# A three-layer transformer on one core: attention results ahead of centring, norm sums by pairs, and the third feed-forward begun on the unnormalised stream

## The chip, the cores and the metric

The kernel runs on one core of one Trainium2 chip. The metric is the device time of one execution in microseconds. The kernel before took 1150.14 us (median of 3 runs, 1149.94 to 1151.73).

## The reference, cut to what matters

Three layers work on one sequence of 256 tokens with width 1024, in float32. The first two are alike (`first_block`), the third is another kind (`second_block`):

```python
# first_block, twice
h = rmsnorm(x, norm_mix[l]);  proj = h @ w_in[l]
# ... attention over selected keys, HGRN recurrence, gates ...
x = x + merged @ w_out[l]
h = rmsnorm(x, norm_ffn[l])
g, u = jnp.split(h @ w_ffn_in[l], 2, axis=-1)
x = x + (jax.nn.silu(g) * u) @ w_ffn_out[l]

# second_block, once
h = rms_norm(x, mix_pre_g[i]) * (1.0 + sc1) + sh1
y = hybrid_mixer(h, ...)   # concat(attention, silu(layer_norm(conv))) @ w_o
x = x + g1 * rms_norm(y, mix_post_g[i])
h = rms_norm(x, ffn_pre_g[i]) * (1.0 + sc2) + sh2
y = swiglu_ffn(h, w_ffn_in[i], w_ffn_out[i])
x = x + g2 * rms_norm(y, ffn_post_g[i])
```

The feed-forward is 2816 wide, which makes 11 slices of 256. A norm's factor `rsqrt(mean(x*x))` belongs to one token, so it can be multiplied in before or after a product over the features; the shift `sh2` can be multiplied with the weights by itself and added afterwards.

## The kernel before, in words

**Units.** All weights pass through TensorE as a list of units, mostly 1024 x 256 weights (1 MB). A unit passes four queues. SyncE loads it into `raw` (6 slots, in the order of the list; a slot is free when `w_lo` of the unit six before is written). ScalarE writes `w_hi`, its rounded high part (`split` on ScalarE), VectorE writes `w_lo`, the rest (`split` on VectorE), each into one of 3 slots, which is free when TensorE has done the unit three before. TensorE then makes three products for each chunk, high by high, high by low and low by high, so as to keep float32's accuracy. The activations are split in the same way (`h_hi`, `h_lo` and so on). All four queues run in program order: `tick()` on ScalarE or VectorE steps to the next unit and splits the one three ahead, `split_ahead()` splits alone, `step()` steps alone. Where these calls stand among the other work is written by hand, and so is TensorE's order.

**Norm sums.** `square` on ScalarE writes the squares of `x` into `h_norm` (8 chunks of 128 features by 256 tokens; each `square` does a pair of chunks). `squares_folded` on VectorE folds 8 chunks to 4 and then to 2 with three additions of 128x512, and `norm_sum` on TensorE sums the two chunks over the partitions with a matrix of ones (`A[0]` gets it). This happens between the first and the second unit of a layer's mixer and its feed-forward. Norms are numbered 0 and 2 (mixers of the first two layers), 1 and 3 (their feed-forwards), 4 (third mixer), 5 (third feed-forward). Unit "ix0", "ix1", "aq0" are a first layer's first three.

**Third mixer's end.** The attention of query tile 1 ends in VectorE's generator `attend`: the inverse row sums, then for two halves of the heads `y = values x inverse` (L1794), then `ya_lo` of both halves (L1798), with `ya_hi` on ScalarE between. The convolution's layer norm runs beside it: the folded sum, the centring `cv - mean` (L2261, released by `c_mu`), squares, a second sum on TensorE (L1038), `rstd`, then `conv_out_hi` and `conv_out_lo` by chunk. The four output units "tout0" to "tout3" (`w_o`) multiply `ya` and `conv_out` into the four banks `A`; bank j holds token tile j // 2 and column half j % 2. `tout0` waits for `ya_lo` of the first half.

**Third feed-forward's start.** When tout3 is done, ScalarE squares each bank (`out_squares`), makes each token tile's factor (`out_factor`), VectorE multiplies with the gain row (`gained_out`, L2279) and adds to the stream (`finished`, L2286), which lies token-major in `x_tm`. ScalarE squares the new stream (`x_squares`), and its factor `rs_x` is multiplied in for all four parts of `x_tm` on VectorE and ScalarE. TensorE turns the result into `A` (`turn_h`, L821), VectorE applies gain and shift, ScalarE makes `h_hi` and VectorE `h_lo`, and TensorE does the first unit, "gate0", pair by pair (`high_parts_first`, L840 to L845). Then come up0, gate1, up1, down0, gate2, up2, down1 and so on. A down unit needs `gu_lo` of its slice, made from `silu(gate) * up`.

Units whose factor and shift are applied afterwards are called `shifted`: they multiply `xs_hi`/`xs_lo`, the gained stream with the shift in two more columns (258 in all). In the kernel before those are the third mixer's first two units.

Of the kernel before, what the change touches and what calls it, by code (L numbers as in the profile page):

```python
# [143 lines left out]
def shifted(u):  # L144
    return u[1] == 2 and u[2] in ("gate0", "val0")
# [48 lines left out]
def build(nc, a, out):  # L194
# [87 lines left out]
    gain_row = [at("mixer_gain_row", [P, D], F32, 159), at("ffn_gain_row", [P, D], F32, 163)]  # L282
    gain_dram = nc.dram_tensor("gain_rows_in_dram", (2, D), F32, kind="Internal").ap()
    xn = at("x_tm_normed", [P, 4, 512], F32, 167)
# [95 lines left out]
    n_fold = Event("norm_squares_folded")  # L380
# [8 lines left out]
    x_scaled, x_sq2, x_ms2 = Event("x_tm_scaled_by_act", 2), Event("x_tm_squares"), Event("x_tm_mean_squares")  # L389
    p_part, x_rs, x_norm, h_turned = Event("out_part", 3), Event("x_tm_rstd"), Event("x_tm_normed_set", 2), Event("h_turned", 4)  # L390
# [123 lines left out]
    def _(sp):  # L514
# [7 lines left out]
        for m in range(2, len(UNITS)):  # L522
# [24 lines left out]
    def _(pe):  # L547
# [33 lines left out]
        def turned(hi, lo, x_h, x_l, k0, first, part):  # L581

            for j in range(4):
# [4 lines left out]
                if part and j < 3:  # L588
                    mm.then_inc(part.sem, 1)
            return mm  # L590

        def stream(count, before=None, between=None):

            for _ in range(count):
# [50 lines left out]
                elif kind == "tout":  # L645
# [3 lines left out]
                    pe.wait_ge(*(y_lo.at(0, name) if name < 2 else c_lo.at(0, k0 + 1)))  # L649
                    mm = turned(hi, lo, y_h, y_l, k0, name == 0, p_part if name == 3 else None)  # L650
# [54 lines left out]
        def norm_sum(ni):  # L705
            pe.wait_ge(*n_fold.at(ni))
# [108 lines left out]
        def turn_h(half):  # L815

            pe.wait_ge(*x_norm.at(0, half))
            pe.wait_ge(*x_scaled.at(0, half))
            for k in range(4 * half, 4 * half + 4):
                for t in range(NT):  # L820
                    mm = pe.transpose(A[k // 2][:, T * (k % 2) + P * t:T * (k % 2) + P * t + P],  # L821
                                      xn[:, 2 * t + half, P * (k % 4):P * (k % 4) + P], ident)
                if k % 2:
                    mm.then_inc(h_turned.sem, 1)

        def high_parts_first():
# [3 lines left out]
            pe.wait_ge(*lo_at(m))  # L830
            for e, c in BANKS[m][1]:
# [3 lines left out]
            for j in range(4):  # L835
                pairs = [(n, k) for n in range(2) for k in (2 * j, 2 * j + 1)]
                pe.wait_ge(*n_hi.at(NTH_NORM[5], j))
                for n, k in pairs:
                    out, ws = bank(m)[:, T * n:T * n + T], (slice(None), k, slice(P * n, P * n + P))
# [1558 lines left out]
```

## Time and profile before

| | |
|---|---|
| median of 3 runs | 1150.14 us |
| the profiled execution's own time | 1151.75 us |
| its span, first to last instruction | 1149.7 us |
| TensorE busy | 1113.0 us, 97% |
| VectorE busy | 861.6 us, 75% |
| ScalarE busy | 622.6 us, 54% |
| mean granted TensorE clock | 0.992 |

The span is what the trace shows; 2.05 us of the profiled execution lie outside it. PE is TensorE, PEld its weight loads, DVE VectorE, ACT ScalarE, SPq the DMA queue that SyncE issues to. All ScalarE work carries the line of one helper, so it is told apart by its tiles.

### The profile page before, as it was taken

How to read it: one execution, taken by the hardware profiler on the slowest of the kernel's cores; microseconds unless marked ns; L12 is line 12 of the kernel's file. 1: busy time of each engine (PE TensorE's matmuls, PEld its weight loads, DVE VectorE, ACT ScalarE, POOL GpSimd, SP SyncE). 2: the span in 40 equal slices, each digit the busy share in tenths (PEclk: the TensorE clock that was granted, in tenths of full speed). 3: DMA queues.
4: the chain of work that ended last, by engine and by line, in shares of the span. 5: the costliest groups of instructions: out<-in, count | busy, mean ns of one | idle time of the engine just before them, and what ended most of it. 6: DMA issues, size and time to landing. Idle time of an engine off the chain costs nothing.

```text
span 1149.7 us, 20164 instructions
## 1 busy us (share of the span) xinstructions
PE 1113.0 (97%) x8452; PEld 1065.2 (93%) x8452; DVE 861.6 (75%) x1357; ACT 622.6 (54%) x780; POOL 0.2 (0%) x4
## 2 busy tenths in 40 slices
PE   5999999999999999999999999999999988999997
PEld 5899999999999998999999999999998868999997
DVE  7997766777988877986767788898699966545444
ACT  7677465554444356584664644344588576334333
POOL 0000000000000000000000000000000000000000
PEclk9999999999999999999999999999999998999999
DMA  9646444747879554564346568796555154555520
GB/s 345 210 147 186 145 147 144 254 153 261 278 249 318 164 169 149 156 199 157 122 135 227 193 224 280 245 316 209 160 148 176 43 185 147 184 184 183 184 74 37
DMA packets 176394, 215.14 MB, mean 187 GB/s; under 512 B 5808, under 2 KB 157744, under 8 KB 176304
## 3 DMA queue, kind: packets, MB, share of 16 engines
q1 hardware_dynamic: 175616, 213.20, 56.8%
q8 instruction: 67, 1.10, 0.4%
q10 hardware_dynamic: 688, 0.66, 0.2%
q14 instruction: 23, 0.19, 0.0%
HBM read 212.79 MB, written 1.06 MB: 186 GB/s over the span
## 4 chain that ended last, share of the span: by engine, by line
PE 76%; DVE 17%; ACT 5%; issue 2%; DMA 1%; DVEq 0%; ACTq 0%
PE stream L552 16%; PE stream L554 16%; PE stream L553 16%; DVE w_lo L1583 6%; PE steps L552 6%; PE steps L553 6%; PE steps L554 6%; ACT w_hi L1054 2%; PE stream L636 1%; PE stream L638 1%; PE stream L637 1%; DVE conv_acc L2166 1%; PE steps L966 1%; PE stream L804 1%; DVE conv_acc L2180 1%
## 5 line engine op out<-in xcount | busy, mean ns | idle before, releaser
L1583 DVE TENSOR_TENSOR w_lo<-raw,w_hi 128x2048 fp32r<-128x2048 f32 (+2 forms) x178 | 401.3, 2265 | 175.4 <-ACT w_hi L1054 174.4
L1054 ACT ACTIVATE w_hi<-raw 128x2048 fp32r<-128x2048 f32 (+2 forms) x178 | 336.3, 1893 | 285.3 <-PE stream L554 247.7
L552 PE MATMUL stream<-h_hi,w_hi 128*128 128x256 f32 x1592 | 455.3, 286 | 3.3 <-DVE w_lo L1583 3.0
L553 PE MATMUL stream<-h_lo,w_hi 128*128 128x256 f32 x1592 | 450.4, 283 | 0.0
L554 PE MATMUL stream<-h_hi,w_lo 128*128 128x256 f32 x1592 | 450.4, 283 | 0.0
L552 PEld LDWEIGHTS stream<-h_hi,w_hi 128*128 128x128 f32 x1592 | 305.2, 192 | 7.8 <-DVE w_lo L1583 5.1
L553 PEld LDWEIGHTS stream<-h_lo,w_hi 128*128 128x128 f32 x1592 | 305.4, 192 | 1.4 <-issue 1.0
L554 PEld LDWEIGHTS stream<-h_hi,w_lo 128*128 128x128 f32 x1592 | 305.3, 192 | 0.0
L552 PE MATMUL steps<-gu_hi,w_hi 128*128 128x256 f32 x352 | 99.9, 284 | 0.2 <-DVE gu_lo L1885 0.2
L553 PE MATMUL steps<-gu_lo,w_hi 128*128 128x256 f32 x352 | 99.6, 283 | 0.0
L554 PE MATMUL steps<-gu_hi,w_lo 128*128 128x256 f32 x352 | 99.6, 283 | 0.0
L1853 DVE SCALAR_TENSOR_TENSOR ada_sum<-ada_raw,c_act,ada_sum 128x256 f32<-128x256 f32 x168 | 81.5, 485 | 6.0
L1054 ACT ACTIVATE gu_hi<-gu 128x512 fp32r<-128x512 f32 x33 | 20.9, 632 | 101.4 <-DVE gu L1881 101.4
L552 PEld LDWEIGHTS steps<-gu_hi,w_hi 128*128 128x128 f32 x352 | 67.5, 192 | 0.4 <-issue 0.4
L553 PEld LDWEIGHTS steps<-gu_lo,w_hi 128*128 128x128 f32 x352 | 67.5, 192 | 0.0
L554 PEld LDWEIGHTS steps<-gu_hi,w_lo 128*128 128x128 f32 x352 | 67.5, 192 | 0.0
L636 PE MATMUL stream<-w_hi,h_hi 128*128 128x512 f32 (+1 forms) x152 | 59.3, 390 | 1.7 <-DVE w_lo L1583 1.7
L638 PE MATMUL stream<-w_lo,h_hi 128*128 128x512 f32 (+1 forms) x152 | 58.1, 382 | 0.0
L637 PE MATMUL stream<-w_hi,h_lo 128*128 128x512 f32 (+1 forms) x152 | 58.0, 382 | 0.0
L1885 DVE TENSOR_TENSOR gu_lo<-gu,gu_hi 128x512 fp32r<-128x512 f32 x33 | 22.8, 692 | 23.0 <-ACT gu_hi L1054 23.0
L552 PE MATMUL stream<-x_gained_hi,w_hi 128*128 128x256 f32 x128 | 36.8, 287 | 0.9 <-DVE x_gained_lo L1632 0.9
L636 PEld LDWEIGHTS stream<-w_hi,h_hi 128*128 128x128 f32 x152 | 29.2, 192 | 7.7 <-DVE w_lo L1583 2.3
(367 smaller groups left out, 1620.0 us busy)
## 6 DMA issues: line engine op xcount, KB each, us to landing
raw<-in_w_ffn_in SPq DMA_DIRECT2D x66, 1024.0 KB, 5.7
raw<-in_w_in SPq DMA_DIRECT2D x54, 1024.0 KB, 5.4
raw<-in_w_ffn_out SPq DMA_DIRECT2D x33, 1024.0 KB, 5.1
ada_raw<-in_ada_w SPq DMA_DIRECT2D x24, 1024.0 KB, 6.4
raw<-in_w_out SPq DMA_DIRECT2D x8, 1024.0 KB, 5.1
raw<-in_w_proj_attn SPq DMA_DIRECT2D x8, 512.0 KB, 3.5
raw<-in_w_proj_hgrn SPq DMA_DIRECT2D x8, 512.0 KB, 4.5
raw<-in_w_o SPq DMA_DIRECT2D x4, 1024.0 KB, 4.9
```

Source lines behind the costliest of these rows:

```text
L552: pe.matmul(dst, w_h, x_h, start=start, stop=False, skip_group_check=True)
L553: pe.matmul(dst, w_h, x_l, start=False, stop=False, skip_group_check=True)
L554: return pe.matmul(dst, w_l, x_h, start=False, stop=stop, skip_group_check=True)
L636: pe.matmul(dst, h_h[:, k0 + k, ts], hi[:, k, :], start=k0 + k == 0, stop=False)
L637: pe.matmul(dst, h_l[:, k0 + k, ts], hi[:, k, :], start=False, stop=False)
L638: mm = pe.matmul(dst, h_h[:, k0 + k, ts], lo[:, k, :], start=False, stop=k0 + k == KC - 1)
L804: mm = pe.matmul(conv_bank[:, 0:T], diag[j], upad[:, 3, j:j + T], start=j == 0, stop=j == PE_TAPS - 1)
L966: mm = pe.matmul(level_bank(i)[:, c, :], kp[i % 2][:, c, :], qp[:, c, :].rearrange("p (n two h) -> p n two h", two=2, h=h)[:, :, 1, :], st ...
L1054: return act.activation(out_, in_, func, **kw)
L1583: tt(wl[m % SPL][:, 0:n], raw[m % RAW][:, 0:n], wh[m % SPL][:, 0:n].bitcast(F32), ALU.subtract)\
L1853: ins = stt(acc, w[:, k, :], cact[:, k:k + 1], acc, ALU.mult, ALU.add)
L1885: tt(gu_l[i % 2].rearrange("p c t -> p (c t)"), gu, gu_h[i % 2].rearrange("p c t -> p (c t)").bitcast(F32), ALU.subtract).then_inc(*lane.m ...
```

## The change

Four places are changed.

1. **Norms 0 and 2.** Four additions of 128x256, one for each pair of squares, replace the three of 128x512, and TensorE sums the four results as they come.
2. **Third mixer.** VectorE does both halves of `y` and `ya_lo` before the centring; a split (of tout1) moves from ahead of them to behind the centring. tout0 does its high parts first and waits for `ya_lo` only ahead of the rest.
3. **Third feed-forward.** gate0 and up0 become shifted units. TensorE turns the new stream itself (`turn_x2`), ScalarE and VectorE make `xs_hi` and `xs_lo` with the gain, and the token factor, spread on VectorE and turned on TensorE, comes afterwards. VectorE makes the normalised `h` from the turned stream (`third_normed`), ScalarE its high part; gate1 is the first unit that uses it. The splits of up0 and gate1 move ahead of the factor on VectorE, that of gate1 ahead of it on ScalarE, and those of up1 and later behind the normalised parts on both.
4. **Memory.** The second gain row moves to where `h_norm` lies, so SyncE's queue also waits for `ya_lo` there.

```diff
 def shifted(u):
-    return u[1] == 2 and u[2] in ("gate0", "val0")
+    return u[1] == 2 and (u[2] in ("gate0", "val0") or u[0] in ("gate", "up") and u[2] == 0)
...
             if m == UOUT[2] + 7:
                 sp.wait_ge(gains_out, 32)
                 sp.wait_ge(*a_pt.upto(2))
+                sp.wait_ge(*y_lo.upto(0))
...
+        def turned_high_first(hi, lo, x_h, x_l, low):
+            parts = [(j, k, slice(P * (j // 2), P * (j // 2) + P), slice(512 * (j % 2), 512 * (j % 2) + 512))
+                     for j in range(4) for k in range(2)]
+            for j, k, ts, ws in parts:
+                pe.matmul(A[j], x_h[:, k, ts], hi[:, k, ws], start=k == 0, stop=False, skip_group_check=True)
+                pe.matmul(A[j], x_h[:, k, ts], lo[:, k, ws], start=False, stop=False, skip_group_check=True)
+            pe.wait_ge(*low)
+            for j, k, ts, ws in parts:
+                mm = pe.matmul(A[j], x_l[:, k, ts], hi[:, k, ws], start=False, stop=False, skip_group_check=True)
+            return mm
...
         def norm_sum(ni):
-            pe.wait_ge(*n_fold.at(ni))
+            if ni in (0, 2):
+                for j in range(4):
+                    pe.wait_ge(*n_pair.at(ni // 2, j))
+                    mm = pe.matmul(A[0][:, 0:T], ones, hn[:, 2 * j, :], start=j == 0, stop=j == 3)
+                mm.then_inc(n_ms.sem, 1)
+                return
...
+        def turn_x2():
+            for j, t, chunks in ((1, 0, range(KC)), (2, 1, range(4)), (3, 1, range(4, KC))):
+                pe.wait_ge(*x2_new.at(0, j))
+                for k in chunks:
                     mm = pe.transpose(A[k // 2][:, T * (k % 2) + P * t:T * (k % 2) + P * t + P],
-                                      xn[:, 2 * t + half, P * (k % 4):P * (k % 4) + P], ident)
+                                      x_tm[:, 2 * t + k // 4, P * (k % 4):P * (k % 4) + P], ident)
...
             if b == 2:
-                turn_h(0)
-                turn_h(1)
+                turn_x2()
                 high_parts_first()
-                stream(3 * FS - 1)
+                turn_rstd()
+                stream(1)
+                stream(1, normed(5))
+                stream(3 * FS - 3)
...
-            for j in range(1, 4):
+            for j in range(3):
                 x_squares(j)
+            for j in range(4):
+                act.wait_ge(*x2_turned.at(0, j))
+                for k in (2 * j, 2 * j + 1):
+                    ins = f(xs_h[:, k, 0:T], A[j][:, T * (k % 2):T * (k % 2) + T], ACT.Copy, scale=gain[:, 1, k:k + 1])
+                    ins.then_inc(*(lane.mark(x_hi) if k % 2 else lane.step()))
+            x_squares(3)
+            tick()
             act.wait_ge(*x_ms2.at(0))
...
+            act.wait_ge(*wide_turned.at(0))
+            for t in range(NT):
+                ins = f(rs[:, P * t:P * t + P], bank(UFF[2], t)[:, 3 * P:4 * P], ACT.Copy)
...
             for i in range(FS):
+                for j in range(4 if (b, i) == (2, 0) else 0):
+                    act.wait_ge(*n_hn.at(NTH_NORM[5], j))
+                    for k in (2 * j, 2 * j + 1):
+                        ins = f(hh[:, k, :], hn2[:, k, :], ACT.Identity, bias=mod[:, 3, k:k + 1])
+                        ins.then_inc(*(lane.mark(n_hi) if k % 2 else lane.step()))
                 tick()
-                if scaled_after(UNITS[here()]):
+                if shifted(UNITS[here()]):
+                    shifted_in(sg[0].rearrange("p (c t) -> p c t", c=2), here(), ACT.Silu, g_silu)
+                elif scaled_after(UNITS[here()]):
...
+        act.wait_ge(unit_done, UOUT[2] + 2)
+        shift_hi(1)
         tick(2)
...
         def squares_folded(ni, parts=range(2)):
+            if ni in (0, 2):
+                for j in range(4):
+                    dve.wait_ge(*n_sq.at(ni, j))
+                    tt(hn[:, 2 * j, :], hn[:, 2 * j, :], hn[:, 2 * j + 1, :], ALU.add).then_inc(*lane.mark(n_pair))
+                return
...
+        def third_normed():
+            def low(j):
+                dve.wait_ge(*n_hi.at(NTH_NORM[5], j))
+                for k in (2 * j, 2 * j + 1):
+                    ins = stt(hl[:, k, :], hn2[:, k, :], mod[:, 3, k:k + 1], hh[:, k, :].bitcast(F32), ALU.add, ALU.subtract)
+                    ins.then_inc(*(lane.mark(n_lo) if k % 2 else lane.step()))
+            for k in range(KC):
+                ins = stt(hn2[:, k, :], A[k // 2][:, T * (k % 2):T * (k % 2) + T], gain[:, 1, k:k + 1], rs, ALU.mult, ALU.mult)
+                ins.then_inc(*(lane.mark(n_hn) if k % 2 else lane.step()))
+                if k % 2 and k > 1:
+                    low(k // 2 - 1)
+            low(3)
...
+                if own:
+                    dve.wait_ge(*n_rs.at(5))
+                    shifted_evac(sg[0].rearrange("p (c t) -> p c t", c=2), 0, True)
+                    third_normed()
                 split_ahead()
...
+                if own:
+                    shifted_evac(gu.rearrange("p (c t) -> p c t", c=2), 1, False)
+                    dve.wait_ge(*lane.last)
+                    for c in range(2):
+                        cs = slice(T * c, T * c + T)
+                        ins = stt(gu[:, cs], gu[:, cs], sbias[:, 1, c:c + 1], sg[0][:, cs], ALU.add, ALU.mult)
...
         next(second)
         step()
-        split_ahead()
-        step()
+        next(second)
         next(second)
         next(second)
         dve.wait_ge(*c_mu.at(0))
         tt(cv, cv, rs.unsqueeze(1).broadcast_to([P, 4, T]), ALU.subtract).then_inc(*lane.mark(c_cen))
-        next(second)
+        split_ahead()
+        step()
...
         parts = [gained_out(0, 0), gained_out(0, 1)]
-        for j in range(2):
-            finished(0, j, parts[j])
+        finished(0, 0, parts[0])
         parts += [gained_out(0, 2), gained_out(0, 3)]
-        for j in range(2, 4):
+        for j in range(1, 4):
             finished(0, j, parts[j])
+        split_ahead()
...
+        for j in range(3):
+            gained_x2_lo(j)
         dve.wait_ge(*x_sq2.at(0))
         tt(rest_x, sum_x[:, 0:4:2], sum_x[:, 1:4:2], ALU.add).then_inc(*lane.mark(x_ms2))
+        gained_x2_lo(3)
         dve.wait_ge(*x_rs.at(0))
+        for t in range(NT):
+            ins = ts_(rs_wide[:, t, :], ones, rs_x[:, t:t + 1], None, ALU.mult)
+            ins.then_inc(*(lane.mark(x_wide) if t else lane.step()))
         tick()
         feed_forward(2)
```

The removed lines between (the scaling of `x_tm`, `affine` and `low`) are those described above; `gained_x2_lo` makes `xs_lo` of a pair from `A`, and `turn_rstd` turns the spread factor into the free columns of gate0's two banks.

## Rows read from the trace of the kernel before

**Rows 1.** TensorE's longest wait after the first unit: total us, times, longest us

```profile
PE steps L821 <- ACT x_tm_normed L1054: 5.8, 1, 5.8
```

**Rows 2.** Timeline around norms 0 and 2: start us, us, instruction, idle before

```profile
15.41 0.16 DVE L2114 CAST pos_f<-pos_i 128x2 f32<-128x2 int32 x1
...
22.16 0.50 PE L636 MATMUL stream<-w_hi,h_hi 128*128 128x512 f32 x1 [1.73 <-DVE w_lo L1583]
...
396.24 0.76 DVE L1677 TENSOR_TENSOR ada_sum_lo<-ada_sum,ada_sum_hi 128x256 fp32r<-128x256 f32 x2
...
422.30 1.28 DVE L1639 TENSOR_TENSOR h_norm<-h_norm 128x512 f32<-128x512 f32 x2
...
424.37 0.70 PE L707 MATMUL steps<-h_norm,ones 128*128 128x256 f32 x2 [1.88 <-DVE h_norm L1642]
...
425.15 0.49 PE L636 MATMUL stream<-w_hi,h_hi 128*128 128x324 f32 x1
...
427.94 0.42 ACT L1054 ACTIVATE rstd<-rstd 128x256 f32<-128x256 f32 x1
...
430.43 0.38 PE L899 MATMUL steps<-consts,rstd 128*128 128x128 f32 x2
```

**Rows 3.** Windows: us, busy us of each engine (count), clock, DMA share, GB/s

```profile
20.00:24.00 4.00, 2.27 (x12) 1.71 (x11) 3.96 (x10) 3.96 (x9) 0.00 (x0) 1.00 1.05 387
...
425.20:429.00 3.80, 3.80 (x17) 3.77 (x16) 3.80 (x8) 3.09 (x4) 0.00 (x0) 0.56 0.31 64
...
924.00:928.00 4.00, 4.00 (x12) 3.15 (x11) 2.49 (x2) 0.40 (x1) 0.00 (x0) 0.58 1.08 317
```

**Rows 4.** Timeline from the last attention results to tout2

```profile
917.72 2.28 DVE L1583 TENSOR_TENSOR w_lo<-raw,w_hi 128x2048 fp32r<-128x2048 f32 x1
...
919.36 1.04 PE L770 MATMUL stream<-probsT,v 128*64 128x128 f32 x16
...
920.45 0.42 DVE L1794 TENSOR_TENSOR y_of_heads<-stream,y_of_heads 128x256 f32<-128x256 f32 x1
...
920.80 1.21 DVE L2261 TENSOR_TENSOR conv_acc<-conv_acc,rstd 128x1024 f32<-128x1024 f32 x1
...
922.49 0.47 PE L552 MATMUL steps<-w_hi,ya_hi 128*128 128x512 f32 x1 [2.08 <-DVE ya_lo L1798]
...
929.63 0.59 PE L1038 MATMUL stream<-scratch,ones 128*128 128x256 f32 x2
...
934.34 0.42 DVE L2273 TENSOR_TENSOR conv_out_lo<-conv_acc,conv_out_hi 128x256 fp32r<-128x256 f32 x1 [0.42 <-ACT conv_out_hi L1054]
```

**Rows 5.** Timeline from the last product of tout3 to down0

```profile
946.17 0.39 PE L554 MATMUL steps<-w_hi,conv_out_lo 128*128 128x512 f32 x1
...
948.49 1.42 DVE L2286 SCALAR_TENSOR_TENSOR xT<-y_gained,rstd_of_token,xT 128x512 f32<-128x512 f32 x2
...
952.32 3.65 PE L821 MATMUL steps<-consts,x_tm_normed 128*128 128x128 f32 x16 [5.76 <-ACT x_tm_normed L1054]
...
955.91 1.00 ACT L1054 ACTIVATE h_norm_third<-steps,mod,gain 128x256 f32<-128x256 f32 x2
...
958.21 1.90 ACT L1054 ACTIVATE w_hi<-raw 128x2048 fp32r<-128x2048 f32 x1
...
962.54 0.28 PE L552 MATMUL stream<-h_hi,w_hi 128*128 128x256 f32 x1
...
979.82 0.40 PE L552 MATMUL steps<-w_hi,gu_hi 128*128 128x512 f32 x1
```

**Rows 6.** Timeline: the third mixer's norm on VectorE; a change of table on ScalarE

```profile
835.98 1.67 DVE L1664 SCALAR_TENSOR_TENSOR h_norm<-xT,gain,rstd 128x256 f32<-128x256 f32 x4
...
842.07 0.88 DVE L1656 SCALAR_TENSOR_TENSOR h_lo<-h_norm,mod,h_hi 128x256 fp32r<-128x256 f32 x2 [0.19 <-ACT h_hi L1054]
...
931.21 1.28 ACT L1054 ACT_TABLE_LOAD   x1
932.50 0.51 ACT L1054 ACTIVATE conv_acc<-conv_acc,params 128x256 f32<-128x256 f32 x1
```

More of the change, by code:

```diff
@@ L813, in turn_x @@
             mm.then_inc(x_turned.sem, 1)
[L815 to L820, printed above, removed]
+        def turn_x2():
+            for j, t, chunks in ((1, 0, range(KC)), (2, 1, range(4)), (3, 1, range(4, KC))):
+                pe.wait_ge(*x2_new.at(0, j))
+                for k in chunks:
                     mm = pe.transpose(A[k // 2][:, T * (k % 2) + P * t:T * (k % 2) + P * t + P],
-                                      xn[:, 2 * t + half, P * (k % 4):P * (k % 4) + P], ident)
-                if k % 2:
-                    mm.then_inc(h_turned.sem, 1)
+                                      x_tm[:, 2 * t + k // 4, P * (k % 4):P * (k % 4) + P], ident)
+                    if t and k % 2:
+                        mm.then_inc(x2_turned.sem, 1)
         def high_parts_first():
@@ L1175, in mixer_out @@
             f(rs_x, rs_x, ACT.Exp, scale=-0.5).then_inc(*lane.mark(x_rs))
-            act.wait_ge(*lane.last)
-            for j in (2, 3):
-                f(xn[:, j, :], x_tm[:, j, :], ACT.Copy, scale=rs_x[:, 1:2]).then_inc(*lane.mark(x_scaled))
-            for j in range(4):
-                if j == 2:
-                    act.wait_ge(*h_turned.at(0, 2))
-                    for k in (4, 5):
-                        f(hn2[:, k, :], A[2][:, T * (k % 2):T * (k % 2) + T], ACT.Identity, scale=gain[:, 1, k:k + 1],
-                          bias=mod[:, 3, k:k + 1]).then_inc(*lane.step())
-                    act.wait_ge(*lane.last)
-                else:
-                    act.wait_ge(*n_hn.at(NTH_NORM[5], j if j < 2 else 2))
-                f(hh[:, 2 * j:2 * j + 2, :], hn2[:, 2 * j:2 * j + 2, :], ACT.Copy).then_inc(*lane.mark(n_hi))
+            act.wait_ge(*wide_turned.at(0))
+            for t in range(NT):
+                ins = f(rs[:, P * t:P * t + P], bank(UFF[2], t)[:, 3 * P:4 * P], ACT.Copy)
+                ins.then_inc(*(lane.mark(n_rs) if t else lane.step()))
         def final_out():
@@ L1564, in _ @@
         mixer_out()
-        tick()
         feed_forward(2)
@@ L1635, in squares_folded @@
         def squares_folded(ni, parts=range(2)):
+            if ni in (0, 2):
+                for j in range(4):
+                    dve.wait_ge(*n_sq.at(ni, j))
+                    tt(hn[:, 2 * j, :], hn[:, 2 * j, :], hn[:, 2 * j + 1, :], ALU.add).then_inc(*lane.mark(n_pair))
+                return
             for i in parts:
@@ L1860, in feed_forward @@
                 step()
-                late = scaled_after(UNITS[here()])
+                late, own = scaled_after(UNITS[here()]), shifted(UNITS[here()])
+                if own:
+                    dve.wait_ge(*n_rs.at(5))
+                    shifted_evac(sg[0].rearrange("p (c t) -> p c t", c=2), 0, True)
+                    third_normed()
                 split_ahead()
@@ L1874, in feed_forward @@
                     dve.wait_ge(*lane.last)
+                elif own:
+                    dve.wait_ge(*g_silu.at(0))
                 else:
@@ L2287, in finished @@
                 .then_inc(*lane.mark(x2_new))
+        dve.wait_ge(unit_done, UOUT[2] + 2)
+        shift_lo(1)
         tick(2)
```

77 lines of the change are left out of this document (37 added, 40 removed).

## The prediction

> **What bounds the kernel now.** I read the page first: TensorE is busy 97% of the span, so time can only come out of its pauses and out of stretches at its lower clock. Then the waits of TensorE alone, over the whole span. After the first unit the longest is 5.8 us, ahead of the third feed-forward [rows 1]; the others that the change touches are 1.88 us at norm 2 and 1.73 us after norm 0 [rows 2], and 2.08 us ahead of tout0 [rows 4]. Third, the windows behind these pauses: the granted clock is 0.56 over 3.80 us after norm 2's, and 0.58 over 4.00 us after tout0's, but 1.00 around the pause of 1.73 us [rows 3]. The two levels are 2.4 and 1.2 GHz, so these two stretches lost 3.80 x 0.44 = 1.67 us and 4.00 x 0.42 = 1.68 us. A pause near 2 us thus costs as much again behind it. Last, the timeline of each place, to see who else holds the end of the wait. Everywhere else TensorE runs without a pause, so what one place gives or takes stays in the end time.
>
> **Norm 2.** The three additions begin at 422.30 and release TensorE at 424.37 [rows 2]. A 128x256 addition takes 0.38 (two take 0.76 [rows 2]), so four end at 422.30 + 1.5 = 423.8. TensorE's four records of the sum take 425.15 - 424.37 = 0.78; after the last pair two are left, 0.4. ix1 starts at 424.2 instead of 425.15. It and its slow stretch took until 430.43, 5.28 us; without the 1.67 us it is 3.61 and ends at 427.8. The turning that follows waits for `rstd`, which ScalarE ends at 427.94 + 0.42 = 428.36, behind two splits and a table load that don't move. So this place gives 430.43 - 428.4 = 2.0 us. I take the full clock because only some 0.5 us of pause are left. Lower bound, clock low as before: 424.2 + 5.28 = 429.5, which gives 0.95. More than 2.0 it can't give.
>
> **Norm 0.** The same additions, so VectorE is 2.04 - 1.5 = 0.55 us earlier at its next instruction (15.41), and from there it works on to the `w_lo` for which TensorE waits until 22.16 [rows 2]. It gives 0.55. But TensorE, done sooner with ix1, pauses longer ahead of 22.16: lower bound -1.1, if a slow stretch of 1.67 us follows that now isn't there. I take 0.55, since the row nearest to it (1.73 us) kept its clock.
>
> **Attention results ahead of centring.** TensorE ends the last values product at 919.36 + 1.04 = 920.4 and then waits until 922.49 [rows 4]. The split at 917.72 no longer stands ahead of half 0, whose `ya_hi` is then written by 920.5, and high parts need no `ya_lo`: tout0 starts at 920.5, and both `ya_lo` (by 921.9) are hidden by its 16 high products. Before, tout0 and its slow stretch took 929.63 - 922.49 = 7.14 us; with no pause ahead of it I take 7.14 - 1.68 = 5.46, which ends at 926.0. What is late next is the second sum (929.63): centring 921.8 to 923.0 (1.21 us [rows 4]), tout1's split 2.28 us to 925.2, two folds of 0.7 and 0.4 us to 926.35. So TensorE waits 0.4 us for it, and the place gives 929.63 - 926.35 = 3.3 us. Behind it everything moves alike: the second `conv_out_lo` is written 934.34 + 0.42 - 929.63 = 5.1 us after the sum, and tout2 comes 5.7 us after it, so 0.6 us of cover is left. tout1's `w_lo` at 925.2 and tout2's at 928.5 are ahead of their units (926.6, 932). `shift_hi` and `shift_lo` are 128x16 and lie in that cover. Bounds: 2.0 if the clock falls all the same (920.5 + 7.14 = 927.6), 3.7 if the sum isn't waited for. SyncE's queue waits for tout1's `w_lo` 5 us longer and for `ya_lo`, which is written by then; up1's weights and the gain rows are needed 14 us later at the earliest. Nothing.
>
> **Third feed-forward.** Times here are from the end of tout3, 946.17 + 0.39 = 946.56 [rows 5]. Before, gate0 ended and up0 started at 962.54, t = 16.0, and down0 at 979.82, t = 33.3; a gate or up unit is (979.82 - 962.54) / 3 = 5.76 us.
>
> - The new stream: its last two parts end at 948.49 + 1.42, t = 3.35. Now three parts stand behind the last `gained_out`, at 2.2, 2.8 and 3.5. TensorE turns from 2.2. After that pause I expect its lower clock (16 turnings took 3.65 us at it [rows 5]); the first pair is turned at about 4.0 (3.7 at full clock).
> - ScalarE: eight chunks from PSUM at 0.45 us (two took 1.00, overlapping [rows 5]), to 7.7; squares 0.65, 8.35; `w_hi` of gate1 1.85 (1.90 [rows 5], less overlap), 10.2; factor, two small instructions, 10.75.
> - VectorE: `w_lo` of up0 3.4 to 5.7; `xs_lo` 4 x 0.9 to 9.5; spreads the factor to 11.2.
> - TensorE: gate0's 32 high products keep pace with ScalarE, 16 low ones follow; with a slow stretch it ends at 11.5, 4.5 us earlier than before. Turning the factor, then up0 11.8 to 17.6.
> - VectorE: `w_lo` of gate1 to 13.45, evacuation of gate0 0.8, `third_normed`. The same work for norm 4 took 835.98 to 842.95, 6.97 us [rows 6]; eight reads from PSUM add some 0.05 each: 7.4, to 21.65. gate1 runs 17.6 to 23.5 with its pairs.
> - **What is late next** is up1's split. ScalarE makes it behind the last `h_hi` (20.7): `w_hi` at 22.55, then `w_lo` 2.28 us to 24.85. TensorE waits 1.35 us; up1 ends at 30.65.
> - ScalarE: table for Silu 1.28, Silu 0.9, `w_hi` of down0, 26.6. VectorE: its `w_lo` to 28.85, evacuation of up0 and two products with bias 1.8 to 30.6; `gu_hi` 0.65, `gu_lo` 0.7: 32.0. TensorE waits 1.35 us more; down0 starts at 32.0. gate2's and up2's `w_lo` (35.3, 37.7) are ahead of their units (37.5, 43.2), so nothing follows.
>
> Of the 4.5 us at gate0 two stalls take 2.7, and some 0.5 go at the factor's turning and gate1's pairs: the place gives 33.3 - 32.0 = 1.3 us. Bounds: 4.3 if neither stall comes (down0 at 11.7 + 17.3 = 29.0); -0.8 if each stall is followed by a slow stretch, the first of which mostly lies in the second wait (0.35), the second of which costs 1.7.
>
> A change of table is followed at once by the next instruction: load at 931.21, 1.28 us, Silu at 932.50 [rows 6]. The Trainium skill ("ScalarE: Activation LUTs", section "What ACT_TABLE_LOAD costs") counts about 1.38 us of drain beside the load for each change of set. The row shows 0.01 us between the load's end and the next instruction, so here the trace doesn't bear it out.
>
> **Sum.** 0.55 + 2.0 + 3.3 + 1.3 = 7.1 us. Against the profiled execution: span 1149.7 to 1142.6, own time 1151.75 to 1144.6. That execution is 1.6 us above the median of the runs shown; from the median, 1150.14 - 7.1 = **1143.0 us**.
>
> **Rivals.**
> - *The lower clock stays or comes back* at one or two of the places (after norm 0, norm 2, at tout0, behind the new stalls). For it: each change leaves some pause, and 1.88 and 2.08 us sufficed. Against: 1.73 us didn't. Each costs 1.1 to 1.7: 1144.3 to 1146.3.
> - *The head start is kept*: if the splits on ScalarE and VectorE are quicker than I count, neither stall comes and the third place gives 4.3: 1140.0. Against it: both engines are booked without a gap from t = 13 on.
> - *A drain at the table*: the wait between load and Silu moves `gu` by 1.38 us, 1144.4. By the skill's section named above this is what a change of set costs.
> - *No change that can be measured*: the change does its steps, but the low stretches come at all four: 1.1 + 1.7 + 1.3 + 2.1 = 6.2 us back, 1149.2.
> - *Slower*: the chain from the last `h_hi` over up1's and down0's splits to `gu_lo` is longer than worked out. It decides when down0 starts later than 33.3 + 5.9 (what the other places give) + 2.3 = t 41.5, 9.5 us later than I count, as with four more splits of 2.28 us in line. If ScalarE and VectorE took turns without overlap in `third_normed` it would be 3.6 us, not enough. At 42.5: 1153.5.
>
> **How the numbers follow.** Chances: forecast 0.49 (own range 1141.8 to 1144.2), clock 0.26, head start 0.08, drain 0.04, no change 0.09, slower 0.04. 0.2% is 2.3 us, about what a measurement of this kernel tells from no change. Faster: 0.49 + 0.26 + 0.08 + 0.04 = 0.87; within 0.09; slower 0.04. The range leaves out most of head start, no change and slower: from 1141.2 (the upper bound of 3.7 at tout0, and norm 0's and the turning's full clock) to 1147.8 (three low stretches).
>
> **What the profile after would show.** TensorE's waits: L821's 5.8 us gone, in its place about 2.2 for the new stream, one of 1.35 for `w_lo` at up1 and one of 1.35 for `gu_lo` at down0; none at tout0, 0.4 at the second sum. Clock 1.00 after norm 2 and in tout0. From the end of tout3: up0 at 11.8, down0 at 32.0. The prediction is wrong if down0 stands at 29 or beyond 34, or if the windows at tout0 still show 0.6.

## The result and the profile after

The changed kernel takes 1143.91 us (median of four, 1142.72 to 1144.48), the kernel before 1150.78 beside it (four, 1149.94 to 1151.73): ratio 0.9944, 95% interval [0.9933, 0.9956], so 6.4 us faster by the ratio. The forecast was 1143.0, range 1141.2 to 1147.8, "faster" at 0.87.

The head of the page of the kernel after: TensorE is still busy for 97% of the span, which is 9.1 us shorter.

```profile
span 1140.6 us, 20223 instructions
PE 1109.9 (97%) x8462; PEld 1061.0 (93%) x8462; DVE 866.3 (76%) x1383; ACT 624.7 (55%) x792; POOL 0.2 (0%) x4
```

TensorE's waits of the kernel after (total us, times, longest us), those that the change touches:

```profile
PE steps L843 <- DVE xT L2357: 2.2, 1, 2.2
PE steps L554 <- DVE gu_lo L1956: 1.4, 2, 1.2
...
PE steps L726 <- DVE h_norm L1677: 1.0, 2, 0.7
...
PE steps L599 <- ACT ya_hi L1086: 0.3, 1, 0.3
```

The 5.8 us of [rows 1] have become 2.2 for the new stream, and a wait of 1.2 for `gu_lo` is new. Norm 2's 1.88 [rows 2] is now 0.30 (the 0.7 is norm 0's, which was 1.38) and the 2.08 ahead of tout0 [rows 4] is 0.3. The windows of the kernel after, which answer to [rows 3]:

```profile
425.20:429.00 3.80, 3.72 (x22) 3.20 (x22) 3.51 (x8) 3.14 (x7) 0.00 (x0) 1.00 0.60 169
920.00:924.00 4.00, 4.00 (x18) 3.12 (x17) 3.96 (x4) 2.32 (x3) 0.00 (x0) 1.00 0.17 33
924.00:928.00 4.00, 4.00 (x19) 3.29 (x18) 3.40 (x6) 3.87 (x8) 0.00 (x0) 1.00 1.06 347
```

The granted clock is 1.00 in both stretches that had 0.56 and 0.58. TensorE's timeline of the kernel after, at the places of [rows 2, 4, 5]:

```profile
20.84 0.50 PE L650 MATMUL stream<-w_hi,h_hi 128*128 128x512 f32 x1 [1.13 <-DVE w_lo L1620]
...
421.70 1.99 PE L726 MATMUL steps<-h_norm,ones 128*128 128x256 f32 x8 [0.30 <-DVE h_norm L1677]
423.35 0.50 PE L650 MATMUL stream<-w_hi,h_hi 128*128 128x324 f32 x1
...
427.34 0.44 PE L931 MATMUL steps<-consts,rstd 128*128 128x128 f32 x2
...
917.66 0.47 PE L599 MATMUL steps<-w_hi,ya_hi 128*128 128x512 f32 x1 [0.26 <-ACT ya_hi L1086]
...
923.24 0.70 PE L1070 MATMUL stream<-scratch,ones 128*128 128x256 f32 x2
...
939.91 0.39 PE L556 MATMUL steps<-w_hi,conv_out_lo 128*128 128x512 f32 x1
942.54 1.98 PE L843 MATMUL steps<-consts,xT 128*128 128x128 f32 x16 [2.24 <-DVE xT L2357]
944.87 0.36 PE L862 MATMUL stream<-x_shifted_hi,w_hi 128*128 128x258 f32 x1 [0.35 <-ACT x_shifted_hi L1086]
...
950.72 0.38 PE L875 MATMUL stream<-consts,rstd_of_rows 128*128 128x128 f32 x2
...
963.39 0.38 PE L554 MATMUL stream<-h_hi,w_hi 128*128 128x256 f32 x1 [0.83 <-DVE w_lo L1620]
...
970.61 0.47 PE L554 MATMUL steps<-w_hi,gu_hi 128*128 128x512 f32 x1 [1.20 <-DVE gu_lo L1956]
```

How far the kernel after is ahead of the kernel before, read down this list against its rows of before:

| point | before | after | ahead | this place gave |
|---|---|---|---|---|
| first unit | 8.53 | 7.41 | 1.12 | (its input landed earlier) |
| layer 1, first unit | 418.75 | 417.67 | 1.08 | about 0.5 from the earlier start, the rest norm 0's |
| after norm 2, the turning | 430.43 | 427.34 | 3.09 | 2.0 |
| second sum | 929.63 | 923.24 | 6.39 | tout0: 3.4 (3.01 ahead at the sum before it) |
| last product of tout3 | 946.17 | 939.91 | 6.26 | |
| down0 | 979.82 | 970.61 | 9.21 | third feed-forward: 2.95 |

The split of the 1.08 comes from other profiles. In three kernels with norm 0 as before, TensorE's first product stood at 7.59 to 7.72, and layer 1 began at 418.21 to 418.37: of the 0.8 to 0.9 us by which they start ahead of the kernel before, 0.4 to 0.5 arrive. The kernel after is 0.5 to 0.7 ahead of those three.

Both profiled executions are far from their medians, on opposite sides: 1151.75 is 1.0 above the one, 1142.72 is 1.2 below the other. That is why they stand 9.0 apart and the medians 6.9.

### The profile page after: what moved, and what is told of

Same layout as the page of the kernel before. It is cut to its first block, busy times and chain, and to the rows that moved or that the text cites. A ratio compares the mean times of both kernels' runs of the same rounds, so it can differ in the third digit from the quotient of the medians.

```text
span 1140.6 us, 20223 instructions
## 1 busy us (share of the span) xinstructions
PE 1109.9 (97%) x8462; PEld 1061.0 (93%) x8462; DVE 866.3 (76%) x1383; ACT 624.7 (55%) x792; POOL 0.2 (0%) x4
## 4 chain that ended last, share of the span: by engine, by line
PE 74%; DVE 16%; ACT 6%; issue 2%; DMA 1%; SPq 0%; DVEq 0%; ACTq 0%
PE stream L554 16%; PE stream L555 15%; PE stream L556 15%; DVE w_lo L1620 6%; PE steps L554 6%; PE steps L555 6%; PE steps L556 6%; ACT w_hi L1086 3%; DVE conv_acc L2237 1%; PE stream L650 1%; PE stream L652 1%; PE stream L651 1%; PE steps L998 1%; DMA raw<-in_w_in 1%; PE stream L827 1%
## 5 line engine op out<-in xcount | busy, mean ns | idle before, releaser
L556 PE MATMUL stream<-h_hi,w_lo 128*128 128x256 f32 x1576 | 445.8, 283 | 0.0
L555 PE MATMUL stream<-h_lo,w_hi 128*128 128x256 f32 x1576 | 445.8, 283 | 0.0
L555 PEld LDWEIGHTS stream<-h_lo,w_hi 128*128 128x128 f32 x1576 | 302.3, 192 | 1.4 <-issue 1.0
L556 PEld LDWEIGHTS stream<-h_hi,w_lo 128*128 128x128 f32 x1576 | 302.2, 192 | 0.0
L555 PE MATMUL stream<-x_gained_lo,w_hi 128*128 128x256 f32 x128 | 36.2, 283 | 0.0
```

The source lines that it names most:

```text
L555: pe.matmul(dst, w_h, x_l, start=False, stop=False, skip_group_check=True)
L556: return pe.matmul(dst, w_l, x_h, start=False, stop=stop, skip_group_check=True)
```

## The experiments

All compare with the kernel before, run on the same chip in the same stretch of runs. Microseconds "by the ratio" are the ratio's distance from 1, times the time before; it follows the means of the runs more than their medians.

### The three parts by themselves

Each of these is the kernel before with one part of the change. The norms:

```
+            if ni in (0, 2):
+                for j in range(4):
+                    pe.wait_ge(*n_pair.at(ni // 2, j))
+                    mm = pe.matmul(A[0][:, 0:T], ones, hn[:, 2 * j, :], start=j == 0, stop=j == 3)
```

> The kernel before with the norm sums of norms 0 and 2 by pairs alone. Theory (the pause at norm 2 and the slow stretch behind it are what it takes away): 2.0 us at norm 2, 0.2 to 0.55 at norm 0, so 2.2 to 2.6 us faster, clock 1.00 in the 4 us after norm 2's sum. Rival (only the pause, not the clock): about 1 us. Rival (hidden again by ScalarE's rstd or a later wait): within 0.5 us of before.

Measured: 1147.95 us, ratio 0.9978 [0.9969, 0.9987], 2.5 us. Attention's results ahead of centring, with `turned_high_first`:

```
+                        pe.wait_ge(*y_hi.at(0, 0))
+                        mm = turned_high_first(hi, lo, y_h, y_l, y_lo.at(0, 0))
...
+        next(second)
...
         tt(cv, cv, rs.unsqueeze(1).broadcast_to([P, 4, T]), ALU.subtract).then_inc(*lane.mark(c_cen))
-        next(second)
+        split_ahead()
+        step()
```

> The kernel before with the attention results ahead of centring and tout0's high parts first, nothing else. Theory: TensorE's pause of 2.08 us ahead of tout0 shrinks to about 0.3 and the low clock behind it goes, 3.3 us faster. Rival (clock falls all the same): 1.7 to 2.0 us. Rival (the second sum waits longer for the centring and takes it back): under 1 us, with a wait of over 1 us ahead of the second sum.

Measured: 1146.86 us, 0.997 [0.9959, 0.9982], 3.5 us. The third feed-forward (everything from `turn_x2` on):

> The kernel before with the third feed-forward's new start alone (with the memory move that it needs). Theory from the changed kernel's trace: down0 starts 2.9 us earlier after tout3's end than before (30.3 against 33.3), so 2.9 us faster in a run whose clock stays up after the new stream's pause of 2.2 us, about 2 where it falls. Theory of the prediction: 1.3 us. Rival (all of gate0's head start of 5 us is kept): 5 us.

Measured: 1147.85 us, 0.9978 [0.9968, 0.9987], 2.5 us, interval 1.5 to 3.7: the prediction's 1.3 us lies below it. So each part is faster by itself. The product of the three ratios is 0.9926, the whole has 0.9944 [0.9933, 0.9956]; with the parts' own intervals that difference isn't settled.

The kernel with the norms alone: TensorE's waits at tout0 and at the norms, then the windows at norm 2 and at tout0:

```profile
PE steps L553 <- DVE ya_lo L1810: 2.1, 1, 2.1
PE steps L710 <- DVE h_norm L1647: 0.3, 1, 0.3
```

```profile
425.20:429.00 3.80, 3.69 (x25) 3.38 (x24) 3.80 (x8) 3.15 (x5) 0.00 (x0) 1.00 0.33 71
920.00:924.00 4.00, 3.38 (x10) 2.73 (x11) 3.51 (x6) 2.34 (x2) 0.00 (x0) 0.70 1.04 347
```

As forecast: pause gone and clock full at norm 2, pause and low clock left at tout0. The kernel with the attention part alone says something else. Its waits at norms 0 and 2 (total, times, longest), and its window at norm 2:

```profile
PE steps L722 <- DVE h_norm L1657: 3.4, 2, 1.9
```

```profile
425.20:429.00 3.80, 3.80 (x28) 3.75 (x27) 3.80 (x8) 2.72 (x5) 0.00 (x0) 1.00 0.40 101
```

Norm 2 is as in the kernel before, the pause of 1.9 us is there, and yet the clock is 1.00. In the kernel with the third part alone it is 1.00 there too, with the same pause. That kernel's waits for the new stream and for `gu_lo` are those of the changed kernel:

```profile
PE steps L840 <- DVE xT L2354: 2.2, 1, 2.2
...
PE steps L554 <- DVE gu_lo L1953: 1.4, 2, 1.2
```

A pause of 1.9 us can be followed by the lower clock; it need not be. This also prices the two halves of norm 2's gain apart. The second unit and the turning, with norm 2 as before, in the kernel with the attention part alone:

```profile
424.77 0.50 PE L648 MATMUL stream<-w_hi,h_hi 128*128 128x324 f32 x1
...
428.52 0.38 PE L914 MATMUL steps<-consts,rstd 128*128 128x128 f32 x2
```

From the second unit to the turning it is 3.75 us here and 5.28 in the kernel before [rows 2]: the slow stretch costs 1.5. From layer 1's first unit to the turning it is 10.15 here, 11.68 in the kernel before and 9.67 in the kernel after. So the sum by pairs gives 0.5 us at norm 2 where the clock stayed up anyway, and 2.0 where it had fallen.

### The times fall on steps

Each run's mean granted clock stands beside its time. For the kernel before, all 59 runs of the three calls:

| mean clock | runs | time, us |
|---|---|---|
| 0.996 | 5 | 1147.9 to 1148.1 |
| 0.994 and 0.995 | 28 | 1148.7 to 1150.5 |
| 0.992 | 26 | 1150.7 to 1152.0 |

One slow stretch of [rows 3] lowers the mean clock by about 0.0015 (1.67 us of 1150), and the steps are of about that size, 1.8 us between the middles of the groups. It fits that the same program has none, one or two more such stretches in an execution, by chance; only the profiled executions show where. The fourteen profiles of this study (before, after and the twelve experiments) show them at these places:

| place, and TensorE's pause ahead of it | profiles with this pause, not filled | of these, with the lower clock behind it | what the stretch cost |
|---|---|---|---|
| after norm 0, as before: 1.70 to 1.73 us | 6 | 0 | |
| after norm 0, by pairs: 0.93 to 1.44 us | 8 | 3 | 0.5 us (layer 1 at 418.6 instead of 418.0 to 418.1) |
| norm 2, as before: 1.88 to 1.90 us | 5 | 3 | 1.5 us |
| third mixer, waiting for `k_and_cum`: 1.39 us | 14 | 6 | 0.2 us (33.5 instead of 33.3 to the sum ahead of tout0) |
| tout0, as before: 2.08 us | 4 | 3 | 1.6 us |
| the new stream, before: 5.76 us | 6 | 6 | no profile without to compare |
| the new stream, after: 2.24 us | 7 | 6 | 0.3 to 1.0 us |

Norm 0 by pairs, followed by the lower clock, in the kernel with the early split below (the change with one step moved):

```profile
24.00:28.00 4.00, 4.00 (x16) 3.19 (x15) 3.76 (x9) 1.96 (x3) 0.00 (x0) 0.77 1.05 385
```

So the length of a pause doesn't decide by itself: 1.39 us sufficed in six profiles and 2.08 didn't in one. Nor does every stretch cost the same, since part of the lost time can be waited for anyway. All fourteen profiles have one more stretch behind TensorE's last product, where it has no work left to slow down. The mean clock counts them all alike, so it is a rough guide outside the kernel before: three runs of the third part alone took 1149.1 to 1149.3 us at 0.995, and three took 1147.9 to 1148.1 at 0.994.

The norms alone, at clock 0.996, take 1147.13 to 1147.17: only 0.9 us better than the kernel before at that clock, near what 0.5 us at norm 2 and 0.6 at norm 0 (below) give together. The rest of their 2.5 us goes with having the stretch less often. The changed kernel's runs lie closer together, 1142.7 to 1144.5, at clocks from 0.995 to 1.0. Its lowest is 5.2 us below the lowest of before (1147.9), its median 6.9 below the median. By this reading, which no run shows by itself, some 1.7 us of the gain is one stretch that the median run of before has and the changed kernel hasn't.

### The attention part taken apart

The changed kernel, but tout0 waits for both `ya_lo` ahead of all its products, as before:

```
-                        pe.wait_ge(*y_hi.at(0, 0))
-                        mm = turned_high_first(hi, lo, y_h, y_l, y_lo.at(0, 0))
+                    pe.wait_ge(*(y_lo.at(0, name) if name < 2 else c_lo.at(0, k0 + 1)))
+                    mm = turned(hi, lo, y_h, y_l, k0, name == 0, p_part if name == 3 else None)
```

> The changed kernel, with tout0 waiting for ya_lo ahead of all its products again. Theory: ya_lo of the first half is written 0.6 us after TensorE's present start, so tout0 starts 0.5 us later; of that 0.4 is given back, since the second sum's squares are then no longer late: 0 to 0.5 us slower than the changed kernel. Rival (high parts first carry the gain of this place): 1.5 us slower or more.

Measured: 1143.86 us, 0.995 [0.9938, 0.9962]. And the changed kernel with VectorE's old order (the split ahead of the half results, centring ahead of the second half's `ya_lo`):

```
+        split_ahead()
+        step()
         next(second)
...
-        split_ahead()
-        step()
+        next(second)
```

> The changed kernel, with VectorE's old order (split of tout1 ahead of half 0, centring ahead of ya_lo), and tout0's high parts first kept. Theory: high parts need only ya_hi of half 0, written 0.3 us later behind the split, and ya_lo (1.5 us after it) is hidden by 3.6 us of high products; the centring is 1.1 us earlier. So tout0 starts 0.3 us later and nothing waits at the second sum: within 0.3 us of the changed kernel, which shows that the two halves of this edit each do the same work. Rival (the order carries the gain): 1.5 us slower or more.

Measured: 1143.88 us, 0.9948 [0.9936, 0.9961]. tout0's first product in the former, then in the latter:

```profile
919.46 0.47 PE L554 MATMUL steps<-w_hi,ya_hi 128*128 128x512 f32 x1 [0.95 <-DVE ya_lo L1837]
```

```profile
918.43 0.47 PE L599 MATMUL steps<-w_hi,ya_hi 128*128 128x512 f32 x1 [0.52 <-ACT ya_hi L1086]
```

The pause grows from 0.26 us to 0.95 or 0.52, not to the 2.08 of [rows 4], and the clock stays 1.00 in both profiles. The two edits stand in for each other: either alone takes most of the pause. The medians of the two are 0.6 us above the changed kernel's own of the same call (1143.25), which is less than this measurement can tell; 1.5 us or more, as both rivals had it, isn't borne out.

### The pause filled

To have the pause's clock without its length, the kernel before gets products of `ones` by `ones` ahead of tout0, into a bank that tout0 starts anew; nothing reads them.

```
                         pe.wait_ge(*a_lo.at(2, 0))
+                        for _ in range(FILL):
+                            pe.matmul(A[2][:, 0:T], ones, ones.unsqueeze(1).broadcast_to([P, 2, P]), start=True, stop=True)
```

With `FILL = 8`:

> The kernel before with eight products of ones by ones (128x256, to a bank that nobody reads) in TensorE's pause ahead of tout0, nothing else changed. Theory (half of the place's gain is the clock): the pause is as long, the products fill 1.9 us of it, the granted clock in the 4 us after it is 1.00 instead of 0.58, about 1.5 us faster in the median. Rival (only the pause counts, the clock falls by itself): no change, clock 0.6 after it as before.

Measured: 1150.03 us, ratio 1.0 [0.999, 1.0009]. With `FILL = 4`:

> The kernel before with four products of ones by ones in the pause ahead of tout0 instead of eight. Eight took 3.4 us, longer than the pause of 2.08, and cost 1.2 us of their own; four take 1.7 us and fit. Theory (the low clock behind the pause is half of the place's gain): tout0 starts where it did, clock 1.00 behind it, 1.2 to 1.6 us faster in the median. Rival (only the pause counts): no change.

Measured: 1149.11 us, 0.9985 [0.9977, 0.9994]. The eight products and the first of tout0; then, of the other kernel, the four, and its window:

```profile
919.85 3.72 PE L651 MATMUL steps<-ones 128*128 128x256 f32 x16
923.22 0.59 PE L553 MATMUL steps<-w_hi,ya_hi 128*128 128x512 f32 x1
```

```profile
920.58 1.99 PE L651 MATMUL steps<-ones 128*128 128x256 f32 x8
922.64 0.50 PE L553 MATMUL steps<-w_hi,ya_hi 128*128 128x512 f32 x1
```

```profile
924.00:928.00 4.00, 4.00 (x20) 3.30 (x19) 2.69 (x3) 0.64 (x1) 0.00 (x0) 1.00 1.01 332
```

Eight products take 3.4 us where the pause has 2.08, so tout0 starts 1.2 us late; the clock is full and the two about cancel. Four take 2.0 us and start tout0 on time. That kernel gains 1.7 us by the ratio (interval 0.7 to 2.6), but only 0.9 by the medians, where 1.2 to 1.6 was expected. And that the products held the clock up isn't shown. The kernel of the next section has the same pause, with nothing in it, and its clock is full too:

```profile
919.98 0.47 PE L553 MATMUL steps<-w_hi,ya_hi 128*128 128x512 f32 x1 [2.08 <-DVE ya_lo L1810]
925.50 0.59 PE L1045 MATMUL stream<-scratch,ones 128*128 128x256 f32 x2
```

```profile
924.00:928.00 4.00, 4.00 (x20) 3.31 (x19) 0.91 (x3) 1.82 (x3) 0.00 (x0) 1.00 0.93 325
```

Three of four profiles with the pause empty have the lower clock behind it, neither of the two with it filled: two are too few to tell the products from chance. What is shown is the price of the stretch. From tout0 to the second sum it is 5.52 us here and 7.14 in the kernel before, with the same order and the same pause: 1.6 us. From the convolution's first sum, which TensorE does ahead of tout0 (at 917.28 before, 914.76 here, 914.27 after), to the second it is 12.35 us in the kernel before, 10.74 here, 10.70 with four products and 8.97 in the kernel after. So the attention part gives 1.8 us where the clock stayed up anyway and 3.4 where it had fallen: pause and clock are about half each.

### Norm 2 alone

The pairs at norm 2 only (`PAIRED = (2,)`), to see by difference what norm 0 gives:

> The kernel before with the sum by pairs at norm 2 alone. Theory: norm 0 gives 0.2 to 0.55 us, so this is that much slower than both norms together and 1.7 to 2.3 us faster than before. Rival (norm 0 gives nothing, since its wait is ended by DMA and ScalarE): the same as both together. Rival (the longer pause ahead of aq0 costs clock): faster than both together.

Measured: 1148.29 us, 0.9988 [0.9978, 0.9997]. Both norms had 0.9978 [0.9969, 0.9987] on another chip. The difference, about 1 us for norm 0, lies inside the intervals, so these times decide between none of the three theories. The profiles do better, see norm 0 below.

### The split of up1 made earlier

The prediction's late chain at the third feed-forward begins with ScalarE's `w_hi` of up1 standing behind the four `h_hi`. Here it stands ahead of them:

```
             for i in range(FS):
+                tick()
                 for j in range(4 if (b, i) == (2, 0) else 0):
...
-                tick()
```

> The changed kernel, with ScalarE's split of up1 ahead of the four high parts of the third feed-forward's normalised stream instead of behind them. Theory (ScalarE's order is what makes up1 and down0 wait): ScalarE is idle for 2.5 us there and the split takes 1.9, so up1's wait of 0.83 us and down0's of 1.20 us go, 2.0 us faster than the changed kernel, 8.4 to 9 us faster than before. Rival (VectorE's own chain of w_lo splits and the normalised parts ends last): only up1's wait goes, 0.8 us or less. Rival (the high parts come later and gate1's pairs wait): no faster.

Measured: 1142.69 us (1141.42 to 1142.87), 0.9929 [0.9917, 0.9941]. The same kernel again, in a later call:

> The changed kernel with the early split alone once more, to stand beside the run above on one chip. 1142.7 us as before, 0.6 to 2 us faster than the changed kernel at the same mean clock.

Measured: 1141.56 us, 0.9927 [0.9915, 0.994]. The changed kernel itself again:

> The changed kernel itself, for direct comparison with its variants on one chip. 6.4 to 6.9 us faster than before; its runs stand in steps of about 1.7 us by the mean clock, as those of before do, with fewer low steps.

Measured: 1143.25 us, 0.9944 [0.9932, 0.9957]. And the early split with four products in the pause for the new stream:

```
+            for _ in range(FILL):
+                pe.matmul(bank(UFF[2])[:, 0:T], ones, ones.unsqueeze(1).broadcast_to([P, 2, P]), start=True, stop=True)
             for j, t, chunks in ((1, 0, range(KC)), (2, 1, range(4)), (3, 1, range(4, KC))):
```

> The changed kernel with the split of up1 ahead of the high parts and four products of ones by ones in the pause of 2.2 us ahead of the turning of the new stream, into a bank that gate0 starts anew. Theory (the clock falls behind this pause in most runs and delays the turning): clock 1.00 at the turning, down0 0.5 to 1 us earlier than with the early split alone, mean clock 0.998 or more in most runs. Rival (the low clock there is hidden by ScalarE's pace): the same time as the early split alone.

Measured: 1141.41 us, 0.9926 [0.9913, 0.9938]. Three kernels with the early split give 0.9926 to 0.9929, two of the change as it is 0.9944 and 0.9944: some 1.8 us less, though each pair of intervals still touches. The profiles settle it. From the end of tout3 to down0 it is 29.1 and 28.9 us with the early split, against 31.3 in the changed kernel, all with the lower clock at the turning; at full clock there it is 28.5 (with the four products) against 30.3. That is 1.8 to 2.4 us at this place. The timeline of the kernel with the early split, from the new stream to down0, TensorE and VectorE:

```profile
943.49 3.21 PE L843 MATMUL steps<-consts,xT 128*128 128x128 f32 x16 [2.24 <-DVE xT L2357]
...
970.37 0.47 PE L554 MATMUL steps<-w_hi,gu_hi 128*128 128x512 f32 x1
```

```profile
961.61 2.29 DVE L1620 TENSOR_TENSOR w_lo<-raw,w_hi 128x2048 fp32r<-128x2048 f32 x1
```

VectorE makes up1's `w_lo` straight behind its last `h_lo`, with no idle, and neither up1 nor down0 waits (with the products down0 waits 0.41). Tout3 ends at 941.26 here, so down0 starts at t = 29.1, where the prediction's bound for "neither stall" was 29.0. The time is the best of the study with or without the products in the pause; with them the clock at the turning (944 to 948) was 1.00 instead of 0.57 and down0 0.4 to 0.6 us earlier, which the times don't show; three of the five runs had a mean clock of 0.998 or more. One of seven profiles with this pause left empty has the full clock too, so here as well the products aren't shown to be the cause.

## Why the prediction was right

**The low clock behind a pause.** The prediction took the slow stretches of [rows 3] as the cost of the pauses ahead of them. Half right: they cost 1.5 us at norm 2 and 1.6 at tout0, measured on the same work at either clock, where it had 1.67 and 1.68; and in the changed kernel the two places were followed by 1.00. But whether a pause near 2 us is followed by one is a matter of the execution, which one profile can't tell. It was no argument for norm 0 either that the row of 1.73 us kept its clock: pauses of 1.39 us didn't in six profiles. The profile of before had the stretch at norm 2, at tout0 and at the turning, and took 1151.75 us; set against it, a term with a slow stretch in it is the gain over a bad execution. Taking the sum of 7.1 from the median instead mixed the two.

An estimate from the fourteen profiles, each place's gain with its stretches weighed by how often they came: norm 0 0.5 us (0.65 less 0.5 in three of eight), norm 2 1.4 (0.5, and 1.5 more in three of five), tout0 3.0 (1.8, and 1.6 more in three of four), the third feed-forward 1.8 (the means below), together 6.7; the measured change is 6.4 by the ratio and 6.9 by the medians. So the norm 2 and tout0 terms were some 0.9 too large for a median run and the third feed-forward's 0.5 too small. That the number landed within 0.9 us is in part luck.

**Norm 2**, forecast 2.0, gave 2.0 between the two profiles: second unit at 423.35, `L931` at 427.34, clock 1.00, pause 0.30. Against an execution of before whose clock stayed up it gives 0.5.

**Norm 0**, forecast 0.55 with a bound of -1.1. From ScalarE's squares (11.86 before, 11.18 after) to the first product that waited for `w_lo`, 10.30 us became 9.66, so 0.64 there. Layer 1 has it too. With TensorE's first product at 8.50 to 8.57, three kernels with norm 0 as before begin layer 1 at 418.73 to 418.76; three with the pairs, starting at 8.47 to 8.60 and at full clock, begin it at 418.02 to 418.13. That is 0.6 to 0.7 us. Three more, starting at 8.50 to 8.54, had the lower clock behind the pause, which the bound of -1.1 supposed, and begin it at 418.57 to 418.62: 0.15 us is left.

**tout0**, forecast 3.3, gave 3.4 between the two profiles and 1.8 against full clock. Wrong inside it: TensorE was to start with no pause and then wait 0.4 us at the second sum. It paused 0.26 for `ya_hi`, and at the second sum not at all: VectorE's last fold ended at 923.19, TensorE came at 923.24. The order worked out step by step, half results, centring, split, folds, is what the trace shows.

VectorE's timeline of the kernel after at this place:

```profile
918.36 0.42 DVE L1840 TENSOR_TENSOR ya_lo<-y_of_heads,ya_hi 128x256 fp32r<-128x256 f32 x1 [0.15 <-ACT ya_hi L1086]
918.70 1.22 DVE L2331 TENSOR_TENSOR conv_acc<-conv_acc,rstd 128x1024 f32<-128x1024 f32 x1
919.84 2.28 DVE L1620 TENSOR_TENSOR w_lo<-raw,w_hi 128x2048 fp32r<-128x2048 f32 x1
922.04 0.69 DVE L2335 TENSOR_TENSOR scratch<-scratch 128x512 f32<-128x512 f32 x1
922.76 0.43 DVE L2337 TENSOR_TENSOR scratch<-scratch 128x256 f32<-128x256 f32 x1
```

**The third feed-forward** is the term that was mis-sized: 1.3 forecast, 2.95 between the two profiles. Over all profiles, down0 stands 32.1 to 33.3 us after the end of tout3 with the old start (six, mean 32.7) and 30.3 to 31.3 with the new (five, without the early split, mean 30.8): 1.8 us. Its mechanism was right. The stalls came where they were put, ahead of up1 for `w_lo` (0.83 against 1.35) and ahead of down0 for `gu_lo` (1.20 against 1.35). The times are from the end of tout3, 940.30:

| step | forecast | after |
|---|---|---|
| up0 starts | 11.8 | 10.55 |
| last `h_hi` done, ScalarE begins `w_hi` of up1 | 20.7 | 18.8 |
| `w_lo` of up1 done | 24.85 | 23.0 |
| down0 starts | 32.0 | 30.3 |

ScalarE and VectorE of the kernel after over the same stretch:

```profile
943.89 3.02 ACT L1086 ACTIVATE x_shifted_hi<-steps,gain 128x256 fp32r<-128x256 f32 x8
...
951.13 0.45 ACT L1086 ACTIVATE rstd<-stream 128x128 f32<-128x128 f32 x2 [1.39 <-PE stream L875]
...
959.11 1.90 ACT L1086 ACTIVATE w_hi<-raw 128x2048 fp32r<-128x2048 f32 x1
961.03 1.28 ACT L1086 ACT_TABLE_LOAD   x1
962.32 0.91 ACT L1086 ACTIVATE silu_g<-silu_g,shift_product 128x256 f32<-128x256 f32 x2
```

```profile
953.16 1.66 DVE L1907 SCALAR_TENSOR_TENSOR h_norm_third<-steps,gain,rstd 128x256 f32<-128x256 f32 x4
...
959.24 0.88 DVE L1903 SCALAR_TENSOR_TENSOR h_lo<-h_norm_third,mod,h_hi 128x256 fp32r<-128x256 f32 x2 [0.19 <-ACT h_hi L1086]
961.04 2.29 DVE L1620 TENSOR_TENSOR w_lo<-raw,w_hi 128x2048 fp32r<-128x2048 f32 x1 [0.92 <-ACT w_hi L1086]
...
969.77 0.69 DVE L1956 TENSOR_TENSOR gu_lo<-gu,gu_hi 128x512 fp32r<-128x512 f32 x1 [0.70 <-ACT gu_hi L1086]
```

Two sizes account for the 1.7 us. Up0 came 1.25 earlier. Most of that is the turning at full clock (16 in 1.98 us, not the 3.65 of [rows 5]): in the changed kernel's other profile it ran at the lower clock, and up0 stood at t = 11.64. The rest fits ScalarE's eight chunks, which took 3.02 us, 0.38 each in a row, where I had 0.45 each from a row of two. And `third_normed` took 960.12 - 953.16 = 6.96 us: reading PSUM added nothing to the 6.97 that it costs from SBUF; I had added 0.4. The turning of that other profile:

```profile
943.00 3.63 PE L843 MATMUL steps<-consts,xT 128*128 128x128 f32 x16 [2.23 <-DVE xT L2357]
```

Down0 stood at t = 31.3 there. The price of that stretch is 1.0 us, and the forecast's 32.0 is 0.7 off that execution.

**The rivals.** *Head start kept* was wrong for this kernel, at down0 by 1.3 us, and right for the one with the early split. Its against was too strong: VectorE had 0.92 us idle ahead of up1's `w_lo`, waiting for ScalarE, so the two engines weren't booked without a gap. *Lower clock stays or comes back* happens. Of the changed kernel's two profiles one has it, at the turning, for 1.0 us; its five variants have it there in four, after norm 0 in three and in the third mixer in three, for 0.5 and 0.2 us at the latter two. None has it at norm 2 or tout0. The 1.7 us of the third mixer's stretch shrank to 0.2, and its place has a pause of its own, 1.39 us: the prediction's "Everywhere else TensorE runs without a pause" was not so. *Drain at the table*: the load begins at 961.03 and lasts 1.28 us, Silu begins at 962.32, so 0.01 us between, as in [rows 6]. The Trainium skill ("ScalarE: Activation LUTs", section "What ACT_TABLE_LOAD costs") counts 1.38 us of drain on top; this trace doesn't show it either. *No change* and *slower* didn't come about.

## What to carry to other kernels

Where TensorE is busy 97% of the time, a pause near 2 us can cost 1.5 us more through the clock that follows, but only in some executions. Before a term is taken from one profile, look at the same place in profiles of other executions, price it at either clock, and don't subtract a gain over a bad execution from a median. When an added step lands between two splits of a weight, look which engine idles for the other (here 0.92 us) and put the split that starts the later chain ahead of the work that only feeds the earlier one. Two edits that cut the same pause are priced together: undoing either alone cost 0.6 us by the medians, inside the noise, where the pair gave 1.8 to 3.4. And a run that seems to prove a cause, like the filled pause, needs its empty twin more than once.

## What the runs showed that I hadn't expected

- The times of the kernel before fall on steps about 1.8 us apart that go with the mean clock (0.996, 0.994, 0.992), and a pause of 1.9 us at the same place was followed by 0.56 in some profiles and by 1.00 in others.
- With four products of 128x256 in the pause of 2.08 us the clock was 1.00 and the gain 1.7 us by the ratio, but it was 1.00 in one profile without them too; eight gain nothing, since they take 3.4 us. One such product of f32 data takes 0.42 to 0.5 us, and the trace shows it as two records.
- The lower clock followed a pause of 1.39 us in six of fourteen profiles and cost 0.2 us there.
- A chunk of 128x256 that ScalarE reads from PSUM with a scale per partition takes 0.38 us in a row of eight (3.02).
